# Pooled projections as three-pass tiles ahead of their gates, in a one-core float32 block kernel

## The chip, the cores and the metric

The kernel is one program on one core of a Trainium2 chip. The metric is device time in microseconds of one execution. TensorE (PE) multiplies into PSUM, VectorE (DVE), ScalarE (ACT) and GpSimd (POOL) work elementwise, SyncE (SP) issues most of the weight transfers. Each engine works through its own list of instructions in order and waits at semaphores that the others raise.

## The reference

A sequence of 512 rows with 1024 features passes a differential-attention layer, a gated feed-forward network, a token mixer, and a second gated feed-forward network. The change lies in the mixer. All is float32.

```python
def token_mixer(h, mix_w_in, conv_w, ..., pool_w, pool_scale, pool_proj, dn_proj, mix_w_out):
    xp, q, k, v, z, b_raw, a_raw, g_pool, g_dn = split(h @ mix_w_in)
    pooled = multiscale_pool(xp)                 # 4 groups of 128 columns
    ya = einsum('btgc,gcd->btgd', pooled, pool_w).reshape(B, T, 512) * pool_scale
    ya = ya @ pool_proj                          # 512 x 1024
    qkv = silu(causal_depthwise_conv(concat[q, k, v], conv_w))
    qh, kh = l2_normalize(q part), l2_normalize(k part)      # 8 heads of 128
    o = gated_delta_rule_chunked(qh, kh, vh, g, beta)        # triangular solves, recurrence
    yb = (rms_norm(o) * silu(z)) @ dn_proj
    merged = sigmoid(g_pool) * ya + sigmoid(g_dn) * yb
    return merged @ mix_w_out
```

## The kernel before

Activations lie transposed, features on the partitions and 512 rows on the free axis. A weight tile has 128 output columns. Its blocks come through SP into one of four raw buffers `wr` (a slot, up to 128 x 1024). ACT copies the slot, rounded to TensorE's short float32 format, to `wH`; DVE subtracts and writes the rest to `wL` (both are one `split` step, lines 2078 and 1637; there are three such buffers, so the split of slot j+3 follows the last product of slot j). The other operand is kept as such a pair too (`hH`, `hL`). Each block of 128 input rows is then three rounded passes of 512 columns, on lines 1335, 1336 and 1338: high by high, low by high, high by low. The text below calls those three passes a step. A matrix product of two plain float32 tiles is used where an operand was never split.

One list of steps, written by `Plan.mixer` (line 688), is walked by all engines, each doing its part of every entry. In the mixer the list is paced by a tick, one for each step of products (and, before, one for each product of a projection); other work is hung at given ticks with `at(tick, ...)`. So the place of an entry in each engine's list is set by these numbers.

What stands on the list, with the lines of the profile:

- four pool groups g: DVE pools a tile (`out_pool`), PE multiplies it by `pool_w` (`pool_mid`, line 1456, plain float32), ACT scales the result out of PSUM into `yab` (line 2264);
- `decays` (lines 1927 to 1933 on DVE, 2278 to 2280 on ACT), small vectors of the delta rule;
- k, q and v tiles, eight each: ACT takes a tile from PSUM (line 2293), DVE filters it with four taps (lines 1950 to 1955, `conv_taps`), ACT applies silu, and for k and q squares it and rounds the square (lines 2298, 2305, 2078 to `xr`), DVE makes the rest (line 1637 to `a3r`, `conv_lo`);
- sessions of four heads (`session`): row sums of the squares on PE (lines 1484 and 1485, `l2_sum`), a table load, four logarithms and four exponentials on ACT (2310, 2314, 2318, `l2`), four scalings on DVE (1965, `l2_end`). A k session also has `prep_x` (PE 1499, DVE 1973, ACT 2325 and 2326) and `prep_k` (PE 1506, DVE 1980, then GpSimd); a q session has `prep_q` (PE 1513, DVE 1985 and 1987);
- `solve`: 30 elimination steps on DVE (1996 and 1999), after a transfer through DRAM (`sol_send`) and before one back (`sol_back`); then `inverse`, two groups of small products and copies (PE from line 1521), and the recurrence (`rec_k` line 1574, `rec_v` 1595, `rec_s` 1604, `rec_o` 1614);
- for each of eight column blocks c, a gate tile `gp` (products as above; ACT takes the tanh of it, line 2287, into the one buffer `gpb`) and then `pool_out`: four products of `pool_proj` by `yab` in plain float32 (line 1477), and DVE's (gate + 1) * PSUM into `xT` (line 1939). `pool_proj` comes through GpSimd's queue, two buffers ahead (line 2393).

Of the kernel before, what the change touches and what calls it, by code (L numbers as in the profile page):

```python
# [127 lines left out]
class Plan:  # L128
# [559 lines left out]
    def mixer(self):  # L688
# [15 lines left out]
        def pool_mid(g):  # L704
            add("pool_mid", g=g, bank=wk.take()[1], pm=sig("pm"), ya=sig("ya"), pd=g + 1)
# [159 lines left out]
        def session(end, which, hs):  # L865

            l2s = []
            for j, h in enumerate(hs):
                at(end + 13 + j + (2 if end == 164 else 0), l2_sum, h, l2s)
# [5 lines left out]
            at(end + 17 + (2 if end == 164 else 0), l2, which, l2s)  # L875
            at(end + 26, l2_end, which, l2s)
# [3 lines left out]
        session(120, "q", range(4))  # L880
        session(164, "q", range(4, 8))
# [4 lines left out]
        at(123, lambda: add("sol_send", pa2=8))  # L886
        for k in range(1, 31):
            at(135 + 3 * k, lambda k=k: add("solve", k=k))
        at(227, lambda: add("sol_back"))
        for g in range(2):  # L890
            for j, step in enumerate(("t", "p5", "y5", "p6", "y6")):
                at(251 + 13 * g + 3 * j, inverse, g, step)
        po = iter(range(8))
        for which in "kq":
            for g in range(2):
                for h in range(4 * g, 4 * g + 4):
                    run(conv(which, h))
                run(pool_out(next(po)))
        for h in range(DNH):
            run(conv("v", h))  # L900
            if h % 2:
                run(pool_out(next(po)))
# [48 lines left out]
        add("mix_out", om=self.count["om"], pp=8, m1=8)  # L951
# [47 lines left out]
def model_kernel(nc: bass.Bass, wst, wfd, small_d, const_d, x_d, xd, modd, out_d):  # L999
    plan = Plan()  # L1000
    slots, steps = plan.slots, plan.steps
    place, n_main = {}, 0
    for one in slots:
        if one not in place:
# [3 lines left out]
    with ExitStack() as ctx:  # L1008
# [16 lines left out]
        with ExitStack() as early:  # L1025
            xR = Arena(early, "xr", 4096, F32R)
# [44 lines left out]
        sq3_hi = [xR.t[:, 512 * j:512 * j + 512] for j in range(4, 8)]  # L1071
# [32 lines left out]

        M = ExitStack()
# [14 lines left out]
        sq3_lo = [mR.t[:, 14336 + 512 * j:14848 + 512 * j] for j in range(4)]  # L1120
        Kdr, rB, vB, gpb = [W[:, 0:512], W[:, 512:1024]], yab[0:2], yab[2:4], C("dist")
        Mc = ExitStack()
        A = Arena(Mc, "c3", 2056)
        cr, pool_buf = A.several(2, 516), A.several(2)
# [15 lines left out]
        rhs = {"h": ([c5(hH, c) for c in range(8)], [c5(hL, c) for c in range(8)]), "g": (gH, gL), "o": (oH, oL), "m": (mH, mL)}  # L1140
# [105 lines left out]
        def _(e):  # L1246
# [4 lines left out]
            def weights(j):  # L1251
                n = slots[j][2] * slots[j][4]
                e.dma_start(wr[:, (j % NRAW) * SLOT:(j % NRAW) * SLOT + n],
                            wst[place[slots[j]]:place[slots[j]] + 128 * n].rearrange("(p c) -> p c", p=128)).then_inc(s_raw[j % NRAW], 16)
# [39 lines left out]
        def _(e):  # L1294
# [9 lines left out]
            def ready(t, k):  # L1304
# [8 lines left out]
                elif t.rhs == "o":  # L1313
                    w.wait_ge(s["ol"], k + 1)
                else:
# [28 lines left out]
            for what, d in steps:  # L1344
# [105 lines left out]
                elif what == "pool_mid":  # L1450
                    g = d["g"]
                    b = take(d["bank"])
                    bank_free[d["bank"]] = ("ya", d["ya"])
# [171 lines left out]
        def _(e):  # L1625
# [21 lines left out]
            for what, d in steps:  # L1647
# [286 lines left out]
                elif what == "pool_out":  # L1934
                    if d["k"] == 3:
                        w.wait_ge(s["pp"], d["pp"])
                        w.wait_ge(s["gps"], d["gps"])
                        w.wait_ge(s["saved"], 16)
                        e.scalar_tensor_tensor(X[d["c"]], gpb, 1.0, ps[d["bank"]][:], ALU.add, ALU.mult).then_inc(s["m1"], 1)
# [88 lines left out]
                elif what == "rec_v":  # L2028
                    g, t = d["g"], d["t"]
                    w.wait_ge(s["ur"], d["ur"])  # L2030
                    w.wait_ge(s["pp"], 8)
# [3 lines left out]
                elif what == "rec_s":  # L2035
# [3 lines left out]
                    w.wait_ge(s["pp"], 8)  # L2039
# [34 lines left out]
        def _(e):  # L2074
# [5 lines left out]
            for what, d in steps:  # L2080
# [180 lines left out]
                elif what == "pool_mid":  # L2261
                    g = d["g"]
                    w.wait_ge(s["pm"], d["pm"])
                    e.activation(yab[g], ps[d["bank"]][:], ACT.Copy, scale=S("pool_scale", g, g + 1)).then_inc(s["ya"], 1)
# [122 lines left out]
        def _(e):  # L2387
# [13 lines left out]
            def pool_feed():  # L2401
                if pool_n[0] < len(POOLW):
                    feed(POOLW, pool_buf, s_pool, pool_n[0], pool_at[0])
                    pool_at[0] += 128 * POOLW[pool_n[0]][2] * 128
                    pool_n[0] += 1

            for what, d in steps:
# [46 lines left out]
                elif what == "pool_out":  # L2454
                    if d["k"] == 3:
                        w.wait_ge(s["pp"], d["pp"])
                        pool_feed()
# [88 lines left out]
```

## Time and profile before

| | |
|---|---|
| median of 3 runs (1827.38 to 1829.29) | 1828.8 us |
| the profiled execution | 1829.26 us |
| its span, from which the rows are | 1827.0 us |
| TensorE busy, share of the span | 1803.9 us, 99% |
| DVE, ACT, GpSimd busy | 59%, 46%, 8% |
| granted TensorE clock over the span | 0.999 |
| mixer up to the recurrence's end, about | 960 to 1279 us |

The profiled execution took 2.3 us more than its span and 0.46 us more than the median. PE is busy nearly all the time, so two things can change the time: how long PE's own instructions take, and where it waits for another engine. The list of waits and the rows of the timeline tell the two apart.

### The profile page before, as it was taken

The numbers are of one execution on the slowest core, as the hardware profiler recorded it, in microseconds if no ns is written. First come the engines' busy times: TensorE is split into PE (matmuls) and PEld (weight loads), VectorE is DVE, ScalarE is ACT, GpSimd is POOL, SyncE is SP. The second block draws the span as 40 slices with busy tenths as digits, with TensorE's granted clock in tenths as the row PEclk, the third lists the DMA queues.
The fourth block names the chain that finished last, engine by engine and source line by source line (L and its number), as shares of the span: only waits on it lengthen the run. The fifth ranks groups of instructions, "written<-read, shape, count | busy, mean of one in ns | idle before, by whom it ended". The sixth has DMA issues, their size and how long they took to land.

```text
span 1827.0 us, 21887 instructions
## 1 busy us (share of the span) xinstructions
PE 1803.9 (99%) x8636; PEld 1442.1 (79%) x8636; DVE 1072.8 (59%) x1799; ACT 843.9 (46%) x1371; POOL 141.0 (8%) x159
## 2 busy tenths in 40 slices
PE   8999999999999999999999999999999999999998
PEld 6777777777888788888886877788888878888887
DVE  6777777776525887633348778745434763333323
ACT  5777777777423422222225776335422443222221
POOL 2200000000011022000100120100000100000010
PEclk9999999999999999999999999999999999999999
DMA  5432332323244498533323222310222423322331
GB/s 192 139 104 81 116 104 77 108 93 104 86 156 150 164 324 287 204 97 99 95 80 144 86 84 86 104 59 12 81 93 93 149 88 97 97 99 90 95 96 67
DMA packets 59477, 209.20 MB, mean 115 GB/s; under 512 B 6704, under 2 KB 9136, under 8 KB 58736
## 3 DMA queue, kind: packets, MB, share of 16 engines
q1 hardware_dynamic: 47248, 164.54, 27.3%
q0 software_dynamic: 12128, 43.26, 7.1%
q8 instruction: 69, 1.13, 0.3%
q14 instruction: 32, 0.26, 0.0%
HBM read 202.53 MB, written 5.25 MB: 114 GB/s over the span
## 4 chain that ended last, share of the span: by engine, by line
PE 90%; DVE 6%; ACT 3%; issue 1%; DMA 1%; SPq 0%; DVEq 0%; ACTq 0%
PE ps L1335 24%; PE ps L1338 24%; PE ps L1336 24%; PE ps L1424 2%; PE ps L1448 2%; PE ps L1385 2%; PE ps L1386 2%; PE ps L1392 1%; PE ps L1477 1%; ACT wH L2078 1%; DVE wL L1637 1%; PE ps L1436 1%; DVE b L1717 1%; DMA wr<-wst 1%; DVE gffn L1708 1%
## 5 line engine op out<-in xcount | busy, mean ns | idle before, releaser
L1335 PE MATMUL ps<-hH,wH 128*128 128x512 f32 (+1 forms) x1448 | 577.6, 399 | 1.1 <-DVE hL L1737 1.0
L1637 DVE TENSOR_TENSOR wL<-wr,wH 128x1024 fp32r<-128x1024 f32 (+1 forms) x297 | 360.0, 1214 | 366.3 <-ACT wH L2078 365.7
L1338 PE MATMUL ps<-hH,wL 128*128 128x512 f32 (+1 forms) x1448 | 565.3, 390 | 1.0 <-DVE wL L1637 0.8
L1336 PE MATMUL ps<-hL,wH 128*128 128x512 f32 (+1 forms) x1448 | 563.9, 389 | 0.0
L2078 ACT ACTIVATE wH<-wr 128x1024 fp32r<-128x1024 f32 (+1 forms) x297 | 307.6, 1038 | 236.7 <-PE ps L1338 219.7
L1335 PEld LDWEIGHTS ps<-hH,wH 128*128 128x128 f32 (+1 forms) x1448 | 271.4, 187 | 71.1 <-issue 13.1
L1338 PEld LDWEIGHTS ps<-hH,wL 128*128 128x128 f32 (+1 forms) x1448 | 271.1, 187 | 62.0 <-DVE wL L1637 4.0
L1336 PEld LDWEIGHTS ps<-hL,wH 128*128 128x128 f32 (+1 forms) x1448 | 271.5, 187 | 55.7 <-issue 2.6
L1335 PE MATMUL ps<-gffn,wH 128*128 128x512 f32 (+1 forms) x374 | 142.3, 380 | 0.3 <-DVE xT L1871 0.2
L1338 PE MATMUL ps<-gffn,wL 128*128 128x512 f32 (+1 forms) x374 | 140.9, 377 | 0.0
L1336 PE MATMUL ps<-gffn,wH 128*128 128x512 f32 (+1 forms) x374 | 140.9, 377 | 0.0
L2078 ACT ACTIVATE gffn<-affn 128x512 fp32r<-128x512 f32 x38 | 24.0, 632 | 164.1 <-DVE affn L1863 160.9
L2185 ACT ACTIVATE a<-a,tiny 128x128 f32<-128x128 f32 (+3 forms) x128 | 70.6, 553 | 44.5 <-DVE tiny L1779 44.5
L1335 PEld LDWEIGHTS ps<-gffn,wH 128*128 128x128 f32 x374 | 70.4, 188 | 14.5 <-DVE xT L1871 0.6
L1335 PE MATMUL ps<-g,wH 128*128 128x512 f32 x208 | 81.0, 390 | 0.0
L1338 PE MATMUL ps<-g,wL 128*128 128x512 f32 x208 | 80.9, 389 | 0.0
L1336 PE MATMUL ps<-g,wH 128*128 128x512 f32 x208 | 80.9, 389 | 0.0
L1338 PEld LDWEIGHTS ps<-gffn,wL 128*128 128x128 f32 x374 | 70.4, 188 | 13.0
L1336 PEld LDWEIGHTS ps<-gffn,wH 128*128 128x128 f32 x374 | 70.4, 188 | 13.0 <-issue 0.5
L2242 ACT ACTIVATE affn<-ps 128x512 f32<-128x512 f32 x40 | 23.9, 597 | 109.4 <-PE ps L1338 109.4
L1779 DVE CUSTOM_DVE_ANT_0 a<-ps,a 128x128 f32<-128x128 f32 (+3 forms) x128 | 56.3, 487 | 25.0 <-PE ps L1424 24.9
L1863 DVE TENSOR_TENSOR affn<-ps,affn 128x512 f32<-128x512 f32 x42 | 29.0, 691 | 70.1 <-PE ps L1338 68.4
(337 smaller groups left out, 2356.5 us busy)
## 6 DMA issues: line engine op xcount, KB each, us to landing
wr<-wst SPq DMA_DIRECT2D x280, 512.0 KB, 3.4
fed<-wfd POOLq DMA_DIRECT2D x56, 512.0 KB, 5.2
xT<-wfd POOLq DMA_DIRECT2D x16, 512.0 KB, 4.1
wr<-wst SPq DMA_DIRECT2D x16, 384.0 KB, 3.0
xT<-xin SPq DMA_DIRECT2D x8, 256.0 KB, 7.1
xT<-xin SPq DMA_DIRECT2D x2, 1024.0 KB, 6.1
xsave<-xT SPq DMA_DIRECT2D x1, 2048.0 KB, 7.2
c<-wfd POOLq DMA_DIRECT2D x8, 256.0 KB, 3.4
```

What stands on the lines that cost most here:

```text
L1335: e.matmul(o, hi, vh, start=k == 0, stop=False)
L1336: e.matmul(o, hi, vl, start=False, stop=False)
L1338: i = e.matmul(o, lo, vh, start=False, stop=k == t.nk - 1)
L1385: e.matmul(o, b4(xh[kc], b), hi, start=kc == 0, stop=False)
L1386: e.matmul(o, b4(xl[kc], b), hi, start=False, stop=False)
L1424: i = e.matmul(ps[d["banks"][m]][:, a["at"]:a["at"] + n], qn[h % 2][64 * m:64 * m + 64, 128 * qb:128 * qb + 128], kn[h % 2][64 * m:64 * m ...
L1448: i = e.matmul(b[:, 512 - n:512], b4(oT[h], kb), WT[:, at:at + n], start=kb == 0, stop=kb == 3)
L1637: e.tensor_tensor(dst, x, hi.bitcast(F32), ALU.subtract).then_inc(s[name], 1)
L1779: e.tensor_tensor_reduce(out=Sr[z % 2][:, 512 * m:512 * m + n], in0=ps[d["banks"][m]][:, at:at + n], in1=Th[:, 512 - n:512], scale=-1.0, s ...
L1863: e.tensor_tensor(v, ps[t.bank][:], f["sg"][j % 2], ALU.mult).then_inc(s["fu"], 1)
L2078: e.activation(dst, x, ACT.Copy).then_inc(s[name], 1)
L2185: e.activation(v, v, ACT.Exp, bias=mx[:, m:m + 1], scale=-1.0, accum_out=rsum[:, m:m + 1]).then_inc(s["ex"], 1)
```

## The change

The eight projections `pool_out` become tiles `po` of four blocks whose weights go through the same slots as all others, in three rounded passes. So `pool_mid` leaves a pair: ACT writes the rounded `yH`, and DVE, with an instruction that is new, PSUM * pool_scale - yH into `yL`. ACT copies a finished `po` tile to `xT` (new, `out_po`); the gate's DVE instruction then reads `xT` and writes it in place. `yH` and `yL` lie where the q heads will be, so all eight projections stand before q's first tile: c = 0 behind k heads 0 to 3 and ahead of its gate, c = 1 to 7 in one run behind k heads 4 to 7. The gates follow one by one. The order of the tiles is

- before: k0-3, gp0, po0, k4-7, gp1, po1, q0-3, gp2, po2, q4-7, gp3, po3, v0 v1, gp4, po4, v2 v3, gp5, po5, v4 v5, gp6, po6, v6 v7, gp7, po7
- after: k0-3, po0, gp0, k4-7, po1-7, gp1, q0-3, gp2, q4-7, gp3, v0 v1, gp4, v2 v3, gp5, v4-7, gp6, gp7

q's sessions end at ticks 144 and 184 (120 and 164 before), with row sums 5 and 4 ticks later inside them (0 and 2 before); the elimination steps begin at tick 152 (138), the transfer back at 241 (227), the inverse at 259 (251). The rounded squares move from `xT`'s place to the place of `yab`, so two waits of the recurrence now name the row sums instead of the projections.

```diff
-            add("pool_mid", g=g, bank=wk.take()[1], pm=sig("pm"), ya=sig("ya"), pd=g + 1)
+            add("pool_mid", g=g, bank=wk.take()[1], pm=sig("pm"), ya=sig("ya"), yl=sig("yl"), pd=g + 1)
...
         def pool_out(c):
+            po = sig("po")
+            yield from self.steps_of(Tile("po", src("pool_proj_2", 128 * c, 4), pb.take()[1], "y", ("po", po), c=c, po=po))
+        def pool_gate(c):
             gps = sig("gps")
-            yield from self.steps_of(tile("gp", 4624 + 128 * c, ("gps", gps), c=c, gps=gps))
-            bank, pp, m1 = pb.take()[1], sig("pp"), sig("m1")
-            for k in range(4):
-                add("pool_out", c=c, k=k, bank=bank, pp=pp, m1=m1, gps=gps)
-                yield k
+            yield from self.steps_of(tile("gp", 4624 + 128 * c, ("gps", gps), c=c, gps=gps, po=c + 1, m1=sig("m1")))
...
-        session(120, "q", range(4))
-        session(164, "q", range(4, 8))
+        session(144, "q", range(4))
+        session(184, "q", range(4, 8))
...
-            at(135 + 3 * k, lambda k=k: add("solve", k=k))
+            at(149 + 3 * k, lambda k=k: add("solve", k=k))
...
 # DVE
+                elif what == "pool_mid":
+                    w.wait_ge(s["ya"], d["ya"])
+                    e.scalar_tensor_tensor(yL[g], ps[d["bank"]][:], S("pool_scale", g, g + 1), yH[g].bitcast(F32),
+                                           ALU.mult, ALU.subtract).then_inc(s["yl"], 1)
+                elif what == "out_gp":
+                    w.wait_ge(s["po"], d["po"])
+                    w.wait_ge(s["gps"], d["gps"])
+                    e.scalar_tensor_tensor(v, gpb, 1.0, v, ALU.add, ALU.mult).then_inc(s["m1"], 1)
 # ACT
+                elif what == "out_po":
+                    w.wait_ge(s["slot"], t.done)
+                    e.activation(X[d["c"]], ps[t.bank][:], ACT.Copy).then_inc(s["po"], 1)
 # PE, before the product of block k of a po tile
+                elif t.rhs == "y":
+                    w.wait_ge(s["yl"], k + 1)
```

The instructions of DVE show what the list makes of it at three places. First, around `decays` (the copies to `tiny`), between k heads 0 and 2, before:

```order
L1637 TENSOR_TENSOR wL<-wr,wH 128x1024
L1927 COPY tiny<-ps 128x32
L1928 COPY tiny<-ps 128x32
L1930 TENSOR_TENSOR tiny<-tiny 128x32
L1932 TENSOR_SCALAR tiny<-tiny 128x32
L1933 TENSOR_SCALAR tiny<-tiny 128x32
L1950 TENSOR_SCALAR o<-c,sml 128x512
L1953 SCALAR_TENSOR_TENSOR o<-c,sml,o 128x512 x2
L1955 SCALAR_TENSOR_TENSOR o<-c,sml,o 128x512
L1637 TENSOR_TENSOR a3r<-a,xr 128x512
L1637 TENSOR_TENSOR wL<-wr,wH 128x1024
```

and after (L1936 is `yL`, here the fourth; three others stand ahead of this piece; `o3r` is the new place of the rounded squares):

```order
L1636 TENSOR_TENSOR wL<-wr,wH 128x512
L1926 COPY tiny<-ps 128x32
L1927 COPY tiny<-ps 128x32
L1929 TENSOR_TENSOR tiny<-tiny 128x32
L1931 TENSOR_SCALAR tiny<-tiny 128x32
L1932 TENSOR_SCALAR tiny<-tiny 128x32
L1953 TENSOR_SCALAR o<-c,sml 128x512
L1956 SCALAR_TENSOR_TENSOR o<-c,sml,o 128x512 x2
L1958 SCALAR_TENSOR_TENSOR o<-c,sml,o 128x512
L1636 TENSOR_TENSOR a3r<-a,o3r 128x512
L1636 TENSOR_TENSOR wL<-wr,wH 128x1024
L1936 SCALAR_TENSOR_TENSOR a3r<-ps,sml,a3r 128x512
```

The split ahead of `decays` is now that of the first projection and half as wide, and the fourth `yL` stands behind the split of gp0's slot. Second, DVE's work of the second k session, before (L1973 is `prep_x`, L1965 `l2_end`, L1950 to L1955 the taps of q0):

```order
L1973 SCALAR_TENSOR_TENSOR a<-ps,tiny,cst 128x128 x4
L1637 TENSOR_TENSOR wL<-wr,wH 128x1024
L1973 SCALAR_TENSOR_TENSOR a<-ps,tiny,cst 128x128 x4
L1950 TENSOR_SCALAR a<-c,sml 128x512
L1953 SCALAR_TENSOR_TENSOR a<-c,sml,a 128x512 x2
L1955 SCALAR_TENSOR_TENSOR a<-c,sml,a 128x512
L1973 SCALAR_TENSOR_TENSOR a<-ps,tiny,cst 128x128 x8
L1965 SCALAR_TENSOR_TENSOR a<-a 128x512 x4
```

and after:

```order
L1976 SCALAR_TENSOR_TENSOR a<-ps,tiny,cst 128x128 x4
L1636 TENSOR_TENSOR wL<-wr,wH 128x1024
L1976 SCALAR_TENSOR_TENSOR a<-ps,tiny,cst 128x128 x8
L1636 TENSOR_TENSOR wL<-wr,wH 128x1024
L1976 SCALAR_TENSOR_TENSOR a<-ps,tiny,cst 128x128 x4
L1968 SCALAR_TENSOR_TENSOR a<-a 128x512 x4
```

The taps are gone from it, since q0 now comes after the seven projections and gp1; a second split stands in it, between the third and the last `prep_x`. Third, DVE ahead of the last row sums of q (the last row is `conv_lo` of q7; 128x220 and the like are elimination steps; L1985 and L1987 `prep_q`), before:

```order
L1985 TENSOR_TENSOR a<-o,a 128x512
L1987 TENSOR_TENSOR a<-ps,a 128x512
L1637 TENSOR_TENSOR a3r<-a,xr 128x512
L1996 TENSOR_TENSOR a<-a 128x220
L1999 TENSOR_TENSOR a<-a 128x11x20
L1996 TENSOR_TENSOR a<-a 128x228
L1999 TENSOR_TENSOR a<-a 128x12x19
L1637 TENSOR_TENSOR wL<-wr,wH 128x1024
L1996 TENSOR_TENSOR a<-a 128x234
L1999 TENSOR_TENSOR a<-a 128x13x18
L1637 TENSOR_TENSOR a3r<-a,xr 128x512
```

and after (L1942 is the gate's instruction, here of gp3):

```order
L1988 TENSOR_TENSOR a<-o,a 128x512
L1990 TENSOR_TENSOR a<-ps,a 128x512
L1999 TENSOR_TENSOR a<-a 128x238
L2002 TENSOR_TENSOR a<-a 128x14x17
L1942 SCALAR_TENSOR_TENSOR xT<-cst,xT 128x512
L1636 TENSOR_TENSOR wL<-wr,wH 128x1024
L1999 TENSOR_TENSOR a<-a 128x240
L2002 TENSOR_TENSOR a<-a 128x15x16
L1636 TENSOR_TENSOR a3r<-a,o3r 128x512
```

Fifteen elimination steps stand ahead of it now, thirteen before, and the gate's instruction too.

## Rows read from the trace of the kernel before

**Rows 1.** The page, busy time of the engines.
```profile
PE 1803.9 (99%) x8636; PEld 1442.1 (79%) x8636; DVE 1072.8 (59%) x1799; ACT 843.9 (46%) x1371; POOL 141.0 (8%) x159
```
**Rows 2.** Waits of PE, 960 to 1290 us: waited for, total, times, longest.
```profile
PE ps L1484 <- DVE a3r L1637: 1.3, 1, 1.3
...
PE ps L1574 <- ACT o L2321: 0.3, 1, 0.3
```
**Rows 3.** Timeline of PE around po0: start, duration, engine, line, operation.
```profile
1004.94 0.39 PE L1335 MATMUL ps<-hH,wH 128*128 128x512 f32 x1
...
1010.15 0.40 PE L1338 MATMUL ps<-hH,wL 128*128 128x512 f32 x1
1010.39 3.60 PE L1477 MATMUL ps<-o,c 128*128 128x512 f32 x8
...
1014.05 0.39 PE L1336 MATMUL ps<-hL,wH 128*128 128x512 f32 x1
```
**Rows 4.** Timeline of ACT, decays to the fourth pool group.
```profile
999.89 0.23 ACT L2278 ACTIVATE tiny<-tiny 128x32 f32<-128x32 f32 x1 [4.14 <-DVE tiny L1930]
...
1003.60 0.58 ACT L2293 ACTIVATE c<-ps 128x512 f32<-128x512 f32 x1
1004.08 1.05 ACT L2078 ACTIVATE wH<-wr 128x1024 fp32r<-128x1024 f32 x1
1005.03 0.68 ACT L2264 ACTIVATE o<-ps,sml 128x512 f32<-128x512 f32 x1
```
**Rows 5.** Timeline of DVE there.
```profile
997.54 0.75 DVE L1955 SCALAR_TENSOR_TENSOR o<-c,sml,o 128x512 f32<-128x512 f32 x1
998.21 1.22 DVE L1637 TENSOR_TENSOR wL<-wr,wH 128x1024 fp32r<-128x1024 f32 x1
```
**Rows 6.** Timeline of ACT, first k session.
```profile
1015.01 0.63 ACT L2078 ACTIVATE xr<-a 128x512 fp32r<-128x512 f32 x1
1015.66 1.28 ACT L2310 ACT_TABLE_LOAD   x1
1016.95 2.42 ACT L2314 ACTIVATE a<-ps,cst 128x512 f32<-128x512 f32 x4
1019.25 2.20 ACT L2318 ACTIVATE a<-a 128x512 f32<-128x512 f32 x4
1022.66 0.63 ACT L2325 ACTIVATE a<-a 128x512 f32<-128x512 f32 x1 [1.21 <-DVE a L1973]
```
**Rows 7.** Timeline of DVE and PE, second k session.
```profile
1066.18 1.12 DVE L1973 SCALAR_TENSOR_TENSOR a<-ps,tiny,cst 128x128 f32<-128x128 f32 x4
...
1072.04 2.48 DVE L1965 SCALAR_TENSOR_TENSOR a<-a 128x512 f32<-128x512 f32 x4
...
1075.46 1.05 PE L1506 MATMUL ps<-a 128*128 128x128 f32 x8
1077.73 1.05 PE L1506 MATMUL ps<-a 128*128 128x128 f32 x8
```
**Rows 8.** Timeline of DVE and PE, second q session.
```profile
1110.07 1.22 DVE L1637 TENSOR_TENSOR wL<-wr,wH 128x1024 fp32r<-128x1024 f32 x1
...
1135.56 0.69 DVE L1637 TENSOR_TENSOR a3r<-a,xr 128x512 fp32r<-128x512 f32 x1
...
1136.39 0.47 PE L1484 MATMUL ps<-xr,rnd 128*128 128x512 f32 x1 [1.28 <-DVE a3r L1637]
```
**Rows 9.** POOL's timeline at the way back, its landing, the inverse's first product.
```profile
1175.14 0.54 POOL L2475 DMA_DIRECT2D dsol<-a  x1 [20.11 <-DVE a L1999]
...
1180.81 1.56 POOL L2478 DMA_DIRECT2D a<-dsol  x2 [0.65 <-issue]
...
a<-dsol POOLq DMA_DIRECT2D x4, 128.0 KB, 3.1
...
L1521 PE MATMUL ps<-cst,a x32: 270/272/273, 1190.9 to 1211.8; 128*128 128x128 f32 x32
```
**Rows 10.** Timeline of ACT, first keys of the recurrence.
```profile
1237.77 2.17 ACT L2352 ACTIVATE a<-ps,tiny 128x128 f32<-128x128 f32 x8
```

More of the change, by code:

```diff
@@ L874, in session @@
                     at(end + 38 + 2 * j, prep_q, h)
-            at(end + 17 + (2 if end == 164 else 0), l2, which, l2s)
+            at(end + 17 + {144: 5, 184: 4}.get(end, 0), l2, which, l2s)
             at(end + 26, l2_end, which, l2s)
@@ L885, in mixer @@
         at(24, pool_mid, 3)
-        at(123, lambda: add("sol_send", pa2=8))
+        at(131, lambda: add("sol_send", pa2=8))
         for k in range(1, 31):
-            at(135 + 3 * k, lambda k=k: add("solve", k=k))
-        at(227, lambda: add("sol_back"))
+            at(149 + 3 * k, lambda k=k: add("solve", k=k))
+        at(241, lambda: add("sol_back"))
         for g in range(2):
             for j, step in enumerate(("t", "p5", "y5", "p6", "y6")):
-                at(251 + 13 * g + 3 * j, inverse, g, step)
-        po = iter(range(8))
+                at(259 + 13 * g + 3 * j, inverse, g, step)
         for which in "kq":
@@ L897, in mixer @@
                     run(conv(which, h))
-                run(pool_out(next(po)))
+                if which == "k":
+                    for c in ((0,), range(1, 8))[g]:
+                        run(pool_out(c))
+                run(pool_gate("kq".index(which) * 2 + g))
         for h in range(DNH):
             run(conv("v", h))
-            if h % 2:
-                run(pool_out(next(po)))
+            for c in {1: (4,), 3: (5,), 7: (6, 7)}.get(h, ()):
+                run(pool_gate(c))
         while events:
@@ L1002, in model_kernel @@
     place, n_main = {}, 0
+    proj_at = {one: 1024 * 9216 + 128 * 128 * 4 + 65536 * c for c, one in enumerate(POOLW[4:])}
     for one in slots:
-        if one not in place:
+        if one not in place and one not in proj_at:
             place[one] = n_main
@@ L1103, in model_kernel @@
             F.close()
+        with ExitStack() as early:
+            o3R = Arena(early, "o3r", 8192, F32R)
+        sq3_hi = [o3R.t[:, 6144 + 512 * j:6656 + 512 * j] for j in range(4)]
         M = ExitStack()
@@ L1120, in model_kernel @@
         sq3_lo = [mR.t[:, 14336 + 512 * j:14848 + 512 * j] for j in range(4)]
+        yH, yL = ([mR.t[:, a + 512 * j:a + 512 + 512 * j] for j in range(4)] for a in (2048, 4096))
         Kdr, rB, vB, gpb = [W[:, 0:512], W[:, 512:1024]], yab[0:2], yab[2:4], C("dist")
@@ L1138, in model_kernel @@
         dsol = nc.dram_tensor("dsol", (4 * 65536,), F32, kind="Internal").ap()
-        rhs = {"h": ([c5(hH, c) for c in range(8)], [c5(hL, c) for c in range(8)]), "g": (gH, gL), "o": (oH, oL), "m": (mH, mL)}
+        rhs = {"h": ([c5(hH, c) for c in range(8)], [c5(hL, c) for c in range(8)]), "g": (gH, gL), "o": (oH, oL), "m": (mH, mL),
+               "y": (yH, yL)}
         g_order = [h for z in range(6) for h in (6 + z, z)] + list(range(12, HEADS))
@@ L2453, in _ @@
                     pool_feed()
[L2454 to L2457, printed above, removed]
                 elif what == "cr_zero":
```

44 lines of the change are left out of this document (15 added, 29 removed).

## Prediction

> **What bounds the kernel now.** I read the page first: PE is busy 1803.9 us of a span of 1827.0 [rows 1], so the time is PE's own work plus what PE waits. The list of PE's waits comes next, for the mixer alone: two matter there, 1.3 us ahead of a row sum of q (L1484, for DVE's `conv_lo`) and 0.3 in the first keys of the recurrence [rows 2]. A shorter product therefore shows in full in the time, and a new wait of PE does too. The timelines then give what an instruction takes and, for DVE and ACT, when each is done beside PE's place; there the reader is to see how near to a wait the other engines already are.
>
> All times below are of the profiled execution (1829.26 us), which is 0.46 above the median of 1828.8.
>
> **PE's own work.** From 1004.94 to 1010.15 PE issues 23 rounded passes, 0.2265 each, so a step of three is 0.68 [rows 3]. The first projection shows eight records on L1477 for four products. From the last pass before it (1010.15) to the second after it (1014.05) are 3.90, less two passes 3.45. As a tile it takes four steps, 2.72. Eight times 0.73 is 5.8 us less. The PE order holds no other product more or less.
>
> **The first projection waits for its fourth low half: +1.6.** Now po0 starts where gp0 did, at 1004.95 (eight steps before 1010.39), and its fourth step, which needs the fourth `yL`, at 1007.0. ACT scaled the fourth group at 1005.03 [rows 4], behind a split at 1004.08, behind 4.14 us in which ACT waited for DVE's small `decays` vectors until 999.89. DVE is the late one, and three `yL` are now ahead of `decays`. Such an instruction with a column as scalar holds DVE 0.67 (997.54 to 998.21 [rows 5]): 2.0 more. The split ahead of `decays` is half as wide, 0.5 less. So ACT moves by 1.5: split 1005.6 to 1006.6, `yH` done at 1007.2. DVE has to make that split's low half first (1.2, until 1007.8), then `yL` (0.75): 1008.5, and PE starts about 0.1 after. The wait is 1.6. Bounds: 0.3, if DVE makes up 1.3 us it has idle; 3, if each new instruction costs the 1.2 of a full split. The row sums of k0 to k3 that follow then stand 0.3 behind what DVE delivers, no wait, 0 to 1.
>
> **The run of seven projections.** A slot lasts 2.7 us here, a usual one 5.4. Each needs a split of 512 columns on ACT and DVE (0.6 each, about half of rows 4 and 5) and a copy of 0.5 on ACT, which has time for that up to the fourth. DVE comes into the run late by what it lost in the first session, so the low half for the fourth is ready at about its need: +0.2 (0 to 1).
>
> The second k session falls on that run. Put the end of k7 on PE at 0. Then po4 ends at 12.2 (16 steps, and three row sums of two passes, 0.45 each). ACT gets to the session's table load only after po4's copy and a split: 12.4 + 0.5 + 0.6. The load is 1.3, the logarithms 2.3, the exponentials 2.2, the first pair for `prep_x` 1.0 [rows 6], a copy 0.5, the split for gp1 1.0: 21.9. DVE: its low half by 23.0, two `prep_x` (1.04 apart, 1.12 long [rows 7]) by 25.2. Then ACT must do two pairs, a copy and q0's split, from 24.2 to 27.8, and only then has DVE that low half (29.0), the last `prep_x` (30.0) and the first of L1965 (0.7): 30.7. PE comes to its first key product after 36 steps, four row sums and four groups of small products. Such a group adds 0.91, by the two of L1506 that lie two steps apart, 2.27 less 1.36 [rows 7]: 24.5 + 1.8 + 3.6 = 29.9. Wait +0.8 (0 to 2). Before, the first of L1965 was done at 1072.8 and PE came at 1075.46 [rows 7], 2.7 spare: this is cover that goes.
>
> The 1.3 for a table load is what the rows show: it starts 0.02 after the instruction before it has ended, takes 1.28, and the first logarithm starts 0.01 behind it [rows 6]. The Trainium skill (ScalarE: Activation LUTs, "What ACT_TABLE_LOAD costs") puts a switch at 2.66 us with a drain. The trace does not agree; by the page the wait would be 2.2 instead of 0.8, and the sum below 0.6 over the time before.
>
> **q's row sums and the elimination.** Before, DVE worked without a gap from the split at 1110.07 to the last `conv_lo` at 1135.56, and PE waited 1.28 for it [rows 8]. PE's place and DVE's work both move. Put the end of the q4 tile at 0. ACT now has the first session's exponentials ahead of q5's copy and split, so DVE starts the same run of work at 9.7. It holds the 25.5 of before, less two elimination steps done by then (1.1), more two at the end (1.6), the four L1965 (2.4, [rows 7]) and the gate of gp3 (0.6): 29.0, and the last `conv_lo` 0.7: 39.4. PE wants it after 44 steps, seven row sums and four groups of 0.91: 29.9 + 3.2 + 3.6 = 36.7. Wait 2.7, that is +1.4 over before. Bounds: -1.4, if none is left; +3, if DVE also waits for ACT.
>
> **Inverse.** The way back took from 1175.14 to 1181.6, where the last of four transfers is issued, and 3.1 to land: 1184.7, while PE came at 1190.9 [rows 9], 6.2 spare. Between the last elimination step and the inverse are now 20 steps (259 less 239), before 26: 4.1 less. DVE is some 2 us further behind PE at that step, because of the later session. That leaves nothing: +0.3 (0 to 2.5).
>
> **Recurrence.** Before, four plain products of po7 (3.45) stood between the last gate's tanh with its split and the first keys. Now nothing does. ACT has the tanh (0.7), a split (1.0), then four scalings of the first group, half of 2.17 [rows 10], done at 2.8 after the gate's end, when PE wants their bank for the second `rec_v` at 1.85 (two groups of keys 0.44 each, one of values 0.97). Wait 1.0, less the 0.3 now [rows 2]: +0.7 (0 to 1.5).
>
> Other edits cost nothing: eight copies and eight half splits more on ACT, and eight low halves and four `yL` on DVE, which are idle 54% and 41% of the span; the cover that is gone is counted above. SP issues eight transfers of 256 KB more and GpSimd eight fewer; each is asked for four slots ahead, and PE shows no wait for a transfer in the mixer [rows 2]. GpSimd's `sol_send` has 21 ticks to the first elimination step, 15 before.
>
> **Sum.** -5.8 + 1.6 + 0.2 + 0.8 + 1.4 + 0.3 + 0.7 = -0.8. From 1829.26 that is 1828.5, and less the 0.46, 1828.0 beside a median of 1828.8. About 0.2% (3.7 us) is what a measurement of this kernel can tell from no change: the forecast is no change.
>
> **Rivals.** *Most waits stay away.* The places are all within 1 to 3 us of no wait; DVE and ACT both have idle time to catch up. Against it: in the first and third place the order leaves no idle time between. With the waits of 1.6 and 2.7 halved and the others gone, the 0.3 of before too, the sum is -5.8 + 0.8 + 0.1 - 0.3 = -5.2, beside the median 1823.6; with no wait at all, also without the 1.3 and 0.3 of before, -7.4: 1821.4. Chance 0.27.
>
> *DVE falls behind through the whole of q.* One mechanism: from q4 to the inverse DVE has no gap, so what it loses there is paid once, at the last row sum or at the inverse. It decides for slower from 4.5 us beyond my 39.4: each of some 28 instructions of full width would have to take 0.16 more, or one more wait for ACT of the size of the 2.4 at 9.7 twice. For it: the tightness; against it: the run of before went at just these durations. Time 1829 + 4 = 1833. Chance 0.10.
>
> *The rounded passes do not go at 0.2265*, because `yH` and `yL` come fresh or the slots are short: then PE's own gain is gone and the time is 1834. Nothing in rows 3 speaks for it, the same pass with other operands keeps its pace; it is within the 0.10.
>
> **Chances and range.** Forecast (1825.2 to 1832.4) 0.63, faster 0.27, slower 0.10. The range of 8 in 10 goes to 1822.8 below, into the first rival, and to 1831.4 above.
>
> **What the new profile would show.** No plain products for the projections; 96 passes with the `y` pair at 0.2265. Among PE's waits: a `po` product for DVE's `yL` of about 1.6; the first key product of k4 for DVE of about 0.8; the row sum of q7 for `conv_lo` of about 2.7; small ones at the inverse and at the second `rec_v`. The forecast is wrong if PE's waits of 960 to 1290 us sum to under 3 or over 10 us; right for the wrong reason if they stand elsewhere.

## The result, and the profile after

The changed kernel takes 1832.19 us (median of 16 executions, 1831.60 to 1833.65), beside 1828.28 for the kernel before (16 executions, 1827.38 to 1829.29). The ratio is 1.0022, 95 % interval 1.0015 to 1.0029: it is slower by 3.9 us, just beyond the 0.2 % that can be told from no change. The forecast was no change, 1828.0 beside 1828.8, and the time lies above its range of 8 in 10, which ends at 1831.4. One execution of all that were taken, in run 6, was slow, 3027.51 us at a granted clock of 0.557; no ratio holds it. The profiled execution of after took 1831.67 us (span 1829.7), that of before 1829.26, so the two traces must explain 2.4 us of the 3.9; the rest is that the first lies 0.5 below its median and the second 1.0 above its own.

PE's busy time fell by 2.9 us against [rows 1], with 32 records more, while the span grew by 2.7:

```profile
PE 1801.0 (98%) x8668; PEld 1448.9 (79%) x8668; DVE 1081.3 (59%) x1811; ACT 852.8 (47%) x1388; POOL 134.8 (7%) x151
```

So the time went into waits. These are PE's in the mixer (line waited for: total, times, longest), to be read against [rows 2], where the two largest of the change's part are 1.3 and 0.3:

```profile
PE ps L1483 <- DVE a3r L1636: 2.4, 1, 2.4
PE ps L1520 <- DMA a<-dsol: 1.7, 1, 1.7
PE ps L1344 <- DVE a3r L1936: 1.4, 1, 1.4
PE ps L1344 <- DVE hL L1736: 1.0, 2, 0.6
PE ps L1594 <- ACT a L2360: 0.9, 1, 0.9
PE ps L1505 <- DVE a L1968: 0.6, 1, 0.6
```

The `hL` row is the same in both. The other five stand where the prediction put them: the row sum of q7, the inverse, the fourth step of po0, the second `rec_v`, the first key product of k4. Together they are 7.0 us (8.0 with `hL`), against 1.6 before: 5.4 more. PE's own work gives back 5.8, so waits and work alone would leave the kernel where it was. Two things are missing from that sum, and the waits' list shows neither.

The first is TensorE's clock. PE's timeline at the row sum of q7 (start, duration, line, operation, idle time before it):

```profile
1148.94 0.39 PE L1347 MATMUL ps<-hH,wL 128*128 128x512 f32 x1
1151.73 0.76 PE L1483 MATMUL ps<-o3r,rnd 128*128 128x512 f32 x1 [2.40 <-DVE a3r L1636]
1152.29 0.63 PE L1484 MATMUL ps<-a3r,rnd 128*128 128x512 f32 x1
1152.72 0.63 PE L1344 MATMUL ps<-hH,wH 128*128 128x512 f32 x1
...
1154.78 0.40 PE L1347 MATMUL ps<-hH,wL 128*128 128x512 f32 x1
```

Behind the wait the passes start 0.43 us apart instead of 0.23. The stretches of the same trace say why (time, busy PE and instructions, granted clock, DMA share, GB/s):

```profile
1144.00:1149.30 5.30, 5.30 (x24) 1.00 0.00 0
1151.70:1154.70 3.00, 2.97 (x7) 0.50 0.55 169
1154.70:1157.70 3.00, 3.00 (x14) 1.00 0.45 158
```

The granted clock stood at 0.50, which is 1.2 GHz, from 1151.28 for 3.41 us, and at 2.4 GHz on both sides. It fell 0.45 us before PE went on, so PE worked 2.96 us at the low clock: the next 30 products took 1.5 us more than at 0.2265 each, on top of the wait of 2.40. (Behind the wait of 1.28 before, where the clock stayed, they took 0.1 more.) The Trainium skill (TensorE: Matmul & The Clock Gate, "Wait — 56ns, not 53.3ns?") gives 426.7 ns from start to start for 512 columns at 1.2 GHz; the trace agrees with 0.43.

The second stands outside the mixer. From 1400 to 1500 us, in the second feed-forward block, PE waits 1.6 us where it waited 0.6 before. Its waits there, in the kernel before and in the changed kernel:

```profile
PE ps L1338 <- DVE wL L1637: 0.4, 1, 0.4
PE ps L1335 <- DVE xT L1871: 0.2, 1, 0.2
```
```profile
PE ps L1344 <- DVE xT L1870: 0.8, 1, 0.8
PE ps L1347 <- DVE wL L1636: 0.8, 2, 0.4
```

The code there is the same in both kernels. The last three experiments below lead to the cause of most of it. With both, the account is -5.8 + 5.4 + 1.5 + 1.0 = +2.1. Laid record against record from the end, PE loses 1.97 over the mixer and 1.03 over the second feed-forward block, 3.0 in all (it came to the mixer 0.41 earlier in the trace of after, so the spans differ by 2.7). The mixer's terms make 1.1 of its 1.97; part of the other 0.9 is that a pass behind a wait is followed after 0.34 instead of 0.23 us, the rest is open.

### The profile page after: what moved, and what is told of

Read it like the earlier page. It is cut to its first block, busy times and chain, and to the rows that moved or that the text cites. A ratio compares the mean times of both kernels' runs of the same rounds, so it can differ in the third digit from the quotient of the medians.

```text
span 1829.7 us, 21982 instructions
## 1 busy us (share of the span) xinstructions
PE 1801.0 (98%) x8668; PEld 1448.9 (79%) x8668; DVE 1081.3 (59%) x1811; ACT 852.8 (47%) x1388; POOL 134.8 (7%) x151
## 3 DMA queue, kind: packets, MB, share of 16 engines
q8 instruction: 69, 1.13, 0.3%
## 4 chain that ended last, share of the span: by engine, by line
PE 85%; DVE 8%; ACT 4%; issue 1%; DMA 1%; POOL 0%; SPq 0%; DVEq 0%; ACTq 0%
PE ps L1344 23%; PE ps L1347 23%; PE ps L1345 23%; PE ps L1433 2%; PE ps L1457 2%; PE ps L1394 2%; PE ps L1395 2%; DVE wL L1636 2%; PE ps L1401 1%; ACT wH L2081 1%; PE ps L1445 1%; DVE b L1716 1%; DVE gffn L1707 1%; PE ps L1423 1%; PE ps L1422 1%
## 5 line engine op out<-in xcount | busy, mean ns | idle before, releaser
L1636 DVE TENSOR_TENSOR wL<-wr,wH 128x1024 fp32r<-128x1024 f32 (+2 forms) x305 | 365.6, 1201 | 370.5 <-ACT wH L2081 369.9
L2081 ACT ACTIVATE wH<-wr 128x1024 fp32r<-128x1024 f32 (+2 forms) x305 | 312.7, 1027 | 233.8 <-PE ps L1347 216.7
```

What stands on the lines that cost most here:

```text
L1636: e.tensor_tensor(dst, x, hi.bitcast(F32), ALU.subtract).then_inc(s[name], 1)
L2081: e.activation(dst, x, ACT.Copy).then_inc(s[name], 1)
```

## The experiments

Each was timed beside the kernel before on the same chip. All but the second, tenth and eleventh start from the changed kernel, and their times stand beside its 1832.2. The mean granted clock of an execution hints at whether the clock fell inside it. In the fourteen traces it is 0.9985 to 0.9991 without a fall (it is then low only for the last 3 to 5 us), 0.9977 to 0.9984 with one of 3.41 us, and 0.9968 in run 1, where it was low for 6.8. On record it has three places, so a single execution can be misread. All 16 executions of the changed kernel have 0.998, and all of the kernel before that were timed beside the experiments 0.999.

**1. q's second row sums four ticks later.**

```diff
-at(end + 13 + j + {144: 5, 184: 4}.get(end, 0), l2_sum, h, l2s)
+at(end + 13 + j + {144: 5, 184: 8}.get(end, 0), l2_sum, h, l2s)
... (the same for l2)
```

> The changed kernel with q's second four row sums four ticks later (2.7 us on PE), so that conv_lo of q7 should be there. In the trace of the changed kernel PE waited 2.4 us there and its granted clock then stood at 1.2 GHz for 3.4 us, some 1.7 us lost. Theory A (one debt): DVE works without a gap from 1122 to 1170 us, so it ends the elimination at the same moment; PE then waits 1.7 + 4.1 = 5.8 us for the way back at the inverse, and the time stays at 1832 (within 1 us). Theory B (separate waits): wait and half clock go, 1832.2 - 4.1 = 1828.1. Theory C (separate waits, the fall of the clock costs nothing): 1832.2 - 2.4 = 1829.8.

Measured: 1835.37 us (1833.94 to 1835.91), ratio to before 1.0038 (1.0024 to 1.0051). None of the three: it is 3.2 slower than the changed kernel. The wait of 2.4 is gone, and a larger one stands at the transposition of v0, for ACT:

```profile
1161.47 1.09 PE L1490 MATMUL ps<-cst,o 128*128 128x128 f32 x4 [4.90 <-ACT o L2306]
```

ACT's timeline shows the way to it. It reaches the logarithms only after the last row sum, and the SiLU of v0 (L2306) is queued behind two table loads, four logarithms and four exponentials:

```profile
1153.60 1.28 ACT L2318 ACT_TABLE_LOAD   x1
1154.89 2.42 ACT L2322 ACTIVATE a<-ps,cst 128x512 f32<-128x512 f32 x4
1157.19 2.20 ACT L2326 ACTIVATE a<-a 128x512 f32<-128x512 f32 x4
1159.41 1.28 ACT L2306 ACT_TABLE_LOAD   x1
1160.70 0.63 ACT L2306 ACTIVATE o<-o 128x512 f32<-128x512 f32 x1
```

Behind that wait the granted clock was 0.50 for 6.8 us. What is put later on PE takes along what other engines do behind it.

**2. The kernel before, the same row sums two ticks earlier.**

```diff
-at(end + 13 + j + (2 if end == 164 else 0), l2_sum, h, l2s)
+at(end + 13 + j + 0, l2_sum, h, l2s)
-at(end + 17 + (2 if end == 164 else 0), l2, which, l2s)
+at(end + 17 + 0, l2, which, l2s)
```

> The kernel before, with q's second four row sums two ticks (1.36 us on PE) earlier, so that its wait there grows from 1.28 to 2.64 us, and nothing else. Theory A (the clock falls behind such a wait): the granted clock drops to 1.2 GHz for some 3.4 us behind it as in the changed kernel, 1828.3 + 1.4 + 1.7 = 1831.4. Theory B (the fall belongs to something else in the changed kernel): clock stays, 1828.3 + 1.4 = 1829.7. Theory C (the wait is hidden by a later one): 1828.3; the inverse had 6.2 us to spare in the kernel before, so no later wait is there to shrink.

Measured: 1831.08 us (1830.06 to 1832.08), ratio 1.0016 (1.0007 to 1.0025): theory A. The wait is 2.60 instead of 1.28, and the clock is halved behind it, in a kernel that has nothing of the change (stretches as above):

```profile
1127.00:1132.70 5.70, 5.70 (x22) 1.00 0.25 78
1135.40:1138.90 3.50, 3.50 (x9) 0.52 0.32 124
1139.00:1142.00 3.00, 3.00 (x15) 1.00 0.00 0
```

So 1.3 us more of a wait cost 2.8. Ten of the 11 executions have 0.998; the one at 0.999 took 1830.06, near theory B's 1829.7.

**3. The inverse three ticks later.**

```diff
-at(259 + 13 * g + 3 * j, inverse, g, step)
+at(262 + 13 * g + 3 * j, inverse, g, step)
```

> The changed kernel with the inverse three ticks later (2.04 us on PE). It waited 1.67 us there for the landing of the way back. Theory A: the wait goes and nothing takes its place, 1832.2 - 1.7 = 1830.5. Theory B: the inverse's second half now stands closer to the recurrence and its products wait for one another without cover, 0.5 to 1.7 given back, 1831.0 to 1832.2. The wait of 2.4 at the row sum of q7 and the clock's fall behind it stay in both.

Measured: 1828.62 us (1828.17 to 1830.31), ratio 1.0003 (0.9994 to 1.0011): 3.6 less than the changed kernel, twice what theory A allows. The inverse's wait is gone (1.7 us), and with it most falls of the clock (1.5 each). In the profiled execution the wait at q7 was 2.41, as long as before, and this time the clock stayed:

```profile
1151.30:1154.30 3.00, 2.99 (x13) 1.00 0.45 156
```

Of the 11 executions, 9 had 0.999 and only two 0.998; those two took 1830.1 and 1830.3, the median of the nine is 1828.5. A wait of 2.4 us is therefore one behind which the clock may fall or not, and a fall costs some 1.5 us. Why the two waits together brought one in every execution and this one alone in two of 11 was not tested. A reading that fits the traces: where the clock doesn't fall at q7, PE comes to the inverse sooner and waits longer there. In the next run, with both waits, it stayed behind 2.41 at q7, and PE then waited 2.25 at the inverse, instead of 1.67, with the fall behind that.

**4. po0 in the run with the others,** its gate's product behind it:

```diff
-for c in ((0,), range(1, 8))[g]:
+for c in ((), range(8))[g]:
     run(pool_out(c))
+    if c == 0:
+        at(clock[0] + 4, lambda: add("gp_mul", c=0, po=1, gps=1))
-session(76, "k", range(4, 8))
+session(72, "k", range(4, 8))
...
-elif what == "out_gp":
+elif what == "gp_mul" or what == "out_gp" and d["c"]:
```

> The changed kernel with the first projection (po0) at the head of the run of the other seven, and the product of its gate with it behind that; the first k group is then followed by its gate alone, k4 to k7 stand four steps earlier, and the second k session with them. Theory A: the wait of 1.4 us for the fourth yL goes, the others stay, 1832.2 - 1.4 = 1830.8. Theory B: DVE had that work queued anyway, and PE waits for the taps or row sums of k4 to k7 instead, 1831.5 to 1833.

Measured: 1832.12 us (1831.01 to 1834.70), ratio 1.0024 (1.0015 to 1.0034): theory B. The 1.4 at po0 and the 0.6 at k4 are gone, and 1.5 stands at the row sums of the first session (0.6 more at the inverse, as just said):

```profile
1015.98 0.47 PE L1485 MATMUL ps<-o3r,rnd 128*128 128x512 f32 x1 [0.81 <-DVE a3r L1638]
1018.09 0.47 PE L1485 MATMUL ps<-o3r,rnd 128*128 128x512 f32 x1 [0.73 <-DVE a3r L1638]
```

DVE's work in the first k group is a debt that PE pays at the first place where it needs DVE.

**5 and 6. The elimination six ticks earlier; and q's row sums later with the transpositions of v0 and v1 later too.**

```diff
-at(149 + 3 * k, lambda k=k: add("solve", k=k))
-at(241, lambda: add("sol_back"))
+at(143 + 3 * k, lambda k=k: add("solve", k=k))
+at(235, lambda: add("sol_back"))
```

> The changed kernel with the elimination and the way back six ticks earlier (two steps of some 0.8 us of DVE each before the gapless stretch that begins at 1122 us, into the two gaps of 2.15 us that DVE has there). Theory A (it is DVE's debt that PE pays at the row sum of q7 and at the inverse): the wait of 2.4 becomes 0.8, the clock no longer falls behind it (1.7), the inverse's 1.7 goes: 1832.2 - 1.6 - 1.7 - 1.7 = 1827.2. Theory B (the elimination isn't what holds DVE up there, the row sum's wait is set by ACT and the taps): no change at the row sum, only the inverse gains, 1830.5. Theory C (as A, but the clock falls somewhere all the same): 1828.9.

Measured: 1828.97 us (1828.05 to 1830.10), ratio 1.0002 (0.9993 to 1.0011). The inverse's wait went, the one at q7 did not:

```profile
PE ps L1483 <- DVE a3r L1636: 2.7, 1, 2.7
```

That is theory B at the row sum, and theory C's time for another reason than C's. Theory A had an error in it: with steps at a fixed pace of one in three ticks, moving them all leaves as many of them among q's last squares as before (nine in the 29 us ahead of the last `conv_lo`, in both traces). Six executions at 0.999 have a median of 1828.6, five at 0.998 one of 1829.7.

```diff
... (the edit of 1)
-at(clock[0] + 15, v_turn, h)
+at(clock[0] + (23 if h < 2 else 15), v_turn, h)
```

> The changed kernel with q's second row sums four ticks later, as in the run before, where PE's wait of 2.4 us went but one of 4.9 came at the transposition of v0 (L1490) for ACT; now the transpositions of v0 and v1 stand eight ticks (5.4 us) later too. Theory A (DVE ends the elimination at the same moment, whatever PE does): both waits go, and the inverse waits 1.7 + 2.4 + 1.7 less some 0.7 that DVE still has idle, about 5; 1831.5. Theory B (no debt, only the order): 1832.2 - 4.1 = 1828.1.

Measured: 1831.68 us (1829.70 to 1834.76), ratio 1.0019 (1.0009 to 1.0028): theory A in its time. The two waits that were moved away came back at the query products (L1512) and at the inverse, with the clock halved behind the second:

```profile
PE ps L1520 <- DMA a<-dsol: 2.2, 1, 2.2
PE ps L1512 <- DVE a L1968: 1.9, 1, 1.9
```

**7 and 8. Both moves, then all of them.** The seventh joins the edits of 5 and 3:

```diff
-at(149 + 3 * k, lambda k=k: add("solve", k=k))
+at(143 + 3 * k, lambda k=k: add("solve", k=k))
... (sol_back as in 5)
-at(259 + 13 * g + 3 * j, inverse, g, step)
+at(262 + 13 * g + 3 * j, inverse, g, step)
```

> The elimination six ticks earlier and the inverse three ticks later, in the changed kernel. Theory A: the inverse has no wait left with the elimination earlier, so its own move adds nothing, 1827.2 as for the elimination alone. Theory B: PE comes to the inverse earlier by what it no longer waits at the row sum, and a wait of 1 to 2 us is left there without the move; then this one is 1 to 2 us faster than the elimination alone, 1826 to 1827.

Measured: 1829.63 us (1827.65 to 1830.29), ratio 1.0004 (0.9995 to 1.0012); its eight executions at 0.999 have a median of 1828.9. Not told from the fifth, as theory A said of the pair; the 2.7 at q7 is in both.

The eighth adds the edit of 4 and puts the first session later:

```diff
-at(end + 13 + j + {144: 5, 184: 4}.get(end, 0), l2_sum, h, l2s)
+at(end + 13 + j + {32: 3, 144: 5, 184: 4}.get(end, 0), l2_sum, h, l2s)
-    at(end + 36 + 2 * j, prep_k, h)
+    at(end + 36 + (3 if end == 32 else 0) + 2 * j, prep_k, h)
... (prep_x and l2 likewise; the edits of 4 and 7)
```

> The elimination earlier, the inverse later, the first projection in the run with the others (where the run of that alone showed its 1.4 us again as 1.5 at the row sums of k2 and k3), and the first session's row sums and products three ticks (2.0 us) later to cover that. Theory A: the 1.4 and the 0.6 at the first key product of k4 go too, 1827.2 - 2.0 = 1825.2, faster than the kernel before. Theory B: DVE's lateness in the first session shows at the next place, the key products or the taps of k4 to k7, and 1 to 2 come back: 1826.5 to 1827.5.

Measured: 1828.53 us (1827.24 to 1830.60), ratio 1.0002 (0.9993 to 1.0011). Theory B, and more than its 1826.5 to 1827.5 (the six executions at 0.999 have a median of 1828.0): the 1.4 came back as 1.2 in the run of projections (L1349 for `wL`) and 0.5 at a row sum.

**9. The elimination paused while q's last squares are made.**

```diff
-at(131, lambda: add("sol_send", pa2=8))
+at(124, lambda: add("sol_send", pa2=8))
-at(149 + 3 * k, lambda k=k: add("solve", k=k))
+at(137 + 3 * k if k < 15 else 198 + (k - 15) * 8 // 3, lambda k=k: add("solve", k=k))
-at(259 + 13 * g + 3 * j, inverse, g, step)
+at(262 + 13 * g + 3 * j, inverse, g, step)
```

> The changed kernel with the elimination begun twelve ticks earlier and then paused from tick 180 to 197, the stretch in which DVE makes the last squares of q (five steps fewer, some 4 us of DVE), and the inverse three ticks later. Moving all steps alike (the run before) took none out of that stretch, and the wait at the row sum of q7 stayed at 2.7. Theory A (the steps among q's last squares make that wait): it goes, the clock does not fall there, and against the 1828.5 that the runs without a fall had with the elimination earlier and the inverse later, 2.4 to 2.7 less: 1826.0, faster than the kernel before. Theory B (the wait is set by ACT's squares, not by DVE): it stays above 2, 1828.5 or, with a fall, 1830. Theory C: the steps put off make the way back late, 2 to 4 us at the inverse: 1828 to 1830.

Measured: 1825.79 us (1825.09 to 1827.58), ratio to before 0.9987 (0.9978 to 0.9996): theory A. In the changed kernel DVE's last `conv_lo` started at 1150.90; here, with no step of the elimination (L1999, L2002) in the 5 us ahead of it, at 1146.92 (the changed kernel first, then this run):

```profile
1150.14 0.40 DVE L1999 TENSOR_TENSOR a<-a 128x240 f32<-128x240 f32 x1
1150.57 0.41 DVE L2002 TENSOR_TENSOR a<-a 128x240 f32<-128x240 f32 x1
1150.90 0.68 DVE L1636 TENSOR_TENSOR a3r<-a,o3r 128x512 fp32r<-128x512 f32 x1
```
```profile
1145.19 0.68 DVE L1942 SCALAR_TENSOR_TENSOR xT<-cst,xT 128x512 f32<-128x512 f32 x1
1145.79 1.22 DVE L1636 TENSOR_TENSOR wL<-wr,wH 128x1024 fp32r<-128x1024 f32 x1
1146.92 0.69 DVE L1636 TENSOR_TENSOR a3r<-a,o3r 128x512 fp32r<-128x512 f32 x1
1147.52 0.40 DVE L1999 TENSOR_TENSOR a<-a 128x240 f32<-128x240 f32 x1
```

and PE waits in the mixer for nothing but the three smaller waits of the changed kernel (`hL` left out):

```profile
PE ps L1344 <- DVE a3r L1936: 1.4, 1, 1.4
...
PE ps L1594 <- ACT a L2360: 0.9, 1, 0.9
PE ps L1505 <- DVE a L1968: 0.6, 1, 0.6
```

All 11 executions have 0.999. Run 3 differs from this one in nothing but the places of the send and the steps, and its wait of 2.41 is gone here.

**10 to 12. The 1.0 us in the second feed-forward block.** Ahead of it the saved x comes back, in two transfers of 1 MB, with weights queued behind. In every trace with the changed plan up to the ninth run ACT waits longer for the first of these weights (7.1 to 7.7 us; 6.3 to 6.5 with the plan of before). The three rows are of the kernel before, the changed kernel and the twelfth run (ACT's first split behind the restore, its idle time and what ended it):

```profile
1419.42 1.06 ACT L2078 ACTIVATE wH<-wr 128x1024 fp32r<-128x1024 f32 x1 [6.46 <-DMA wr<-wst]
```
```profile
1421.62 1.06 ACT L2081 ACTIVATE wH<-wr 128x1024 fp32r<-128x1024 f32 x1 [7.10 <-DMA wr<-wst]
```
```profile
1415.59 1.06 ACT L2083 ACTIVATE wH<-wr 128x1024 fp32r<-128x1024 f32 x1 [6.43 <-DMA wr<-wst]
```

(The "landed" of the expectations is this idle time.) The first try was the number of transfers:

```diff
+if 176 <= j < 184:
+    at = 65536 * (j - 176)
+    e.dma_start(scr[at:at + 65536].rearrange("(p c) -> p c", p=128),
+                wst[at:at + 65536].rearrange("(p c) -> p c", p=128)).then_inc(s["scr"], 16)
```

> The kernel before with eight more transfers of 256 KB on SP's queue (copies within DRAM, behind the weights of eight tiles of the mixer, as many as the projections' slots add in the changed kernel); nothing else. In the traces with the changed plan the weights queued behind the restored x (1412 to 1422 us) landed 7.1 to 7.5 us after their issue, in those with the plan of before 6.4 to 6.5, and DVE's late chain behind them made PE wait some 1.0 us more in the second feed-forward block. Theory A (the number of transfers that went down SP's queue sets it): 7.1 or more here, PE's waits of 1400 to 1500 us rise from 0.6 to 1.6, 1829.3. Theory B (something else in the changed kernel): 6.4 to 6.5, 1828.3.

Measured: 1828.61 us (1828.01 to 1828.97), ratio 1.0001 (0.9992 to 1.0010), ACT idle 6.26: not that. The trace holds the landing of each sixteenth of a transfer. After the issue of the restore's second half, 15 sixteenths of that half had landed by 5.29 us before and 5.22 after, the last at 5.37 and at 6.00. Of the first weights behind it 15 had landed by 6.59 and 6.51, the last at 6.64 and at 7.28, and ACT's split starts 0.02 later. The Trainium skill (DMA: Bandwidth & Descriptors, "Why a DMA increments its semaphore by 16 and not by 1") says that the sixteen engines finish independently and the transfer has landed with the last; the trace agrees. So one part of sixteen was late. What ran beside it shows in the DMA queues from 1416.4 to 1420.4 us of the changed kernel (packets, MB, share of 16 engines):

```profile
q1 hardware_dynamic: 294, 1.48, 94.5%
q8 instruction: 1, 0.02, 1.5%
```

One packet of 16 KB of instructions, 0.95 us long, 2.57 after the issue. That it is PE's program follows from the amount: in the kernel before q8 moved 69 such packets, 1.13 MB, and only PE's list is that long (8636 products and as many weight loads, 65 bytes for each; DVE has 1799 instructions). The trace doesn't name the DMA engine of a packet, so that it held up the late part was a guess, to be tested. In these nine traces it starts 2.6 to 3.7 after the issue, in the three of before and of runs 2 and 10 at 9.4 to 9.6, when the first weights have landed. The last two runs lengthen PE's program, at its start, where it waits anyway:

```diff
 bank_free[5] = ("lam", 3)
+for _ in range(64):
+    e.wait_ge(s["first"], 16)
```

> The kernel before with 64 semaphore waits that are already met, on PE at its start, where it waits 5.0 us for ACT anyway; they only lengthen PE's program. In the trace of before a load of 16 KB of PE's program starts 9.47 us after the issue of the second half of the restored x and takes 1.05; with the changed plan (86 rows more on PE) it starts at 2.6 to 3.7, between that transfer and the weights behind it, and one of the weights' sixteen parts lands 1.1 to 1.6 later than the rest. 64 instructions are 6.9 us of such a program (256 of 64 bytes in some 27.5 us). Theory A (that load is what makes the weights late and PE wait in the second feed-forward block): it moves to 2.6, weights land at 7.1, PE's waits of 1400 to 1500 us rise from 0.6 to 1.6, 1829.4. Theory B (something else): 6.4, 0.6, 1828.4.

Measured: 1828.51 us (1827.79 to 1830.24), ratio 1.0001 (0.9993 to 1.0010). The packet moved by 1.9 only, to 7.55 after the issue, still behind the first weights; ACT's idle time stayed at 6.51. The run didn't bring about what it was to test, and doesn't tell the theories apart.

> The kernel with the pause in the elimination and the later inverse (1825.8), with the same 64 met waits on PE at its start. Theory A: the load of PE's program moves from 3.3 us behind the restore's issue to 3.6 ahead of it, the weights land at 6.4 instead of 7.5, PE's waits of 1400 to 1500 us fall from 2.0 to 0.6, 1825.8 - 1.2 = 1824.6. Theory B (the load has no part in it): landing and waits stay, 1825.8.

Measured: 1824.95 us (1824.47 to 1825.96), ratio 0.9981 (0.9972 to 0.9990): theory A. The packet starts 3.38 ahead of the issue, as forecast, the last sixteenth of the restored x lands at 5.33 instead of the 6.41 of run 9, that of the first weights at 6.61 instead of 7.71, and PE's waits of 1400 to 1500 us are 1.0 instead of 2.0 (run 9 first, then this run):

```profile
PE ps L1344 <- DVE xT L1870: 1.2, 1, 1.2
PE ps L1347 <- DVE wL L1636: 0.8, 2, 0.4
```
```profile
PE ps L1347 <- DVE wL L1638: 0.8, 2, 0.4
PE ps L1344 <- DVE xT L1872: 0.2, 1, 0.2
```

The intervals of runs 9 and 12 overlap, though 7 of the 11 executions here are below the lowest of run 9; it is the trace that tells them apart. The padding by itself did nothing in run 11.

The load explains the wait for `xT` and no more. Of the 1.03 lost in this block by the changed kernel, 0.7 is that wait; the second wait for `wL`, 0.4, is still here. It begins with one DVE instruction (L1858 before, L1859 here), which stands idle for 1.21 us in all ten traces with the changed plan, this one included, and for 0.86 in the four with the plan of before. Why is open. The kernel before, then this run:

```profile
1480.86 0.69 DVE L1858 TENSOR_TENSOR affn<-ps,affn 128x512 f32<-128x512 f32 x1 [0.86 <-ACT affn L2240]
1477.39 0.69 DVE L1859 TENSOR_TENSOR affn<-ps,affn 128x512 f32<-128x512 f32 x1 [1.21 <-ACT affn L2245]
```

This version is faster than both kernels: 3.5 us less than before, 7.2 less than the changed kernel. The gain over before is outside its interval, as that of run 9 is, but at 0.19 % not beyond the 0.2 % of the prediction.

## Why the prediction was wrong

The steps, in its order:

- *PE's own work, -5.8: right.* The passes with the `y` pair start 0.2265 apart without a gap (1045.73 to 1053.89 are 36 passes, 8.16 us).
- *po0's wait for the fourth `yL`, +1.6: right, 1.42.* DVE's `yL` starts at 1007.33, forecast 1007.8.
- *The run of projections, +0.2: none. The first key product of k4, +0.8: 0.6.* The 1.28 of a table load held, so the 2.66 of the page cited in the prediction, and its wait of 2.2, would have been further off.
- *q's row sums, wait of 2.7: 2.4.* The place, the engine and the length were right.
- *The inverse, +0.3: wrong in size, 1.7.* That DVE would be later was counted rightly: from the way back's issue to PE's coming are 10.1 us (1186.83 to 1198.55 less the wait), 15.8 before, 5.7 less where I took 6.1. But the way back took 11.7 from the send's issue to the last landing, where I had reckoned 9.6 from [rows 9]. Of the 2.1 between them 0.5 was there before: the 3.1 is the median of the four transfers, the last of them took 3.6 (the lines on landing below, before and after: shortest, median, longest). The rest came with the change: the send and its landing took 4.2 instead of 3.4, and the last transfer 4.7 instead of 3.6. I took a duration of transfers from one place in time as fixed.

```profile
1186.83 0.55 POOL L2479 DMA_DIRECT2D dsol<-a  x1 [88.42 <-DVE a L2002]
1191.07 2.39 POOL L2482 DMA_DIRECT2D a<-dsol  x3 [3.69 <-DMA dsol<-a]
1193.78 0.78 POOL L2482 DMA_DIRECT2D a<-dsol  x1 [0.32 <-issue]
```
```profile
DMA to landing us min/median/max: 2.9/3.1/3.6
DMA to landing us min/median/max: 2.9/4.6/4.8
```

- *The recurrence, +0.7: right, 0.9 less 0.3.*
- *The sum: wrong.* It priced a wait at its own length. The step that failed is "wait 2.7, that is +1.4 over before": with the clock at 1.2 GHz behind it, it cost 1.5 more in the profiled execution, and run 2 shows the same in the kernel before. (In other executions the fall may have stood behind the inverse's wait, as in run 4; all 16 have the mean clock of one fall.) The inverse's +0.3 was 1.4 too small. And "other edits cost nothing" failed in a place that it did not look at: the 1.0 in the second feed-forward block, 0.7 of it by the place of a load of PE's program, as run 12 shows.

Of the rivals, "most waits stay away" is out: all but one came. "DVE falls behind through the whole of q" gave nearly the right time, 1833, by a mechanism that is not the one seen: DVE was no later than forecast at q7. The mark for being wrong, waits over 10 us in the mixer, was not reached (8.0 with `hL`, which stands in that stretch too), though the time was outside: the waits' list alone can't carry such a mark.

What is shown: the falls of the clock (run 2 against before; the changed kernel against run 3, with the same wait), the elimination's steps as what makes PE wait at q7 (9 against 3), the inverse's wait (3), the load's place (12 against 9). Argued only: that the slower pace behind waits is part of the 0.9 left in the mixer. Not settled: the rest of that 0.9, the 0.36 left in the second feed-forward block, on what it hangs whether the clock falls behind a wait of 2.4, and why the same padding moved the load by 1.9 in one kernel and 6.7 in the other.

## What to carry to other kernels

On an engine that is busy 98 % of the time, price a new wait not by its length alone: look in the trace for what the granted clock does behind the longest wait there is, and ask whether the new one is longer. Where one engine is a debtor, moving its reader, or moving all of its work alike, only moves the wait; what helped was to take work out of the stretch ahead of the deadline and give it back behind. And if a stage slows down whose code is unchanged, look at which transfers, loads of the program too, have come to overlap.

## What was not expected of the hardware

- Behind single waits of PE of 2.2 to 2.7 us the granted clock fell to 1.2 GHz for 3.41 us in some traces and stayed at 2.4 GHz in others (it fell in that of after at 2.40 and stayed in that of run 3 at 2.41); behind the 4.90 of run 1 it stayed low for 6.8. Behind waits of 0.6 to 2.0 us no trace shows a fall.
- A load of 16 KB of PE's program is a packet of 0.88 to 0.95 us in the nine traces in which it ran beside the restored x, and there the last sixteenth of that transfer landed 0.6 to 1.2 us later (6.00 to 6.55 after its issue, 5.37 before); with the load moved away, in run 12, it landed at 5.33.
